# Wide silu columns, half-transfer semaphores and singly loaded modulation tiles at the start of a two-block transformer kernel

## The reference, cut to what matters

```python
mod_lat = split(silu(c) @ ada_w + ada_b, 6)          # six vectors of 1024, from one row c
a_lat = rmsnorm(x, g_pre) * (1 + mod_lat[1]) + mod_lat[0]
b_gate, c_gate, v = split(a_lat @ w_in, 3)            # w_in: 1024 x 3072
y_lat = (b_gate * depthwise_conv3(c_gate * v, conv_w)) @ w_out
x = x + mod_lat[2] * rmsnorm(y_lat, g_post)
f = square(relu(modulate(rmsnorm(x, g_pre_ff), mod_lat[3], mod_lat[4]) @ mlp_w_in)) @ mlp_w_out
x = x + mod_lat[5] * rmsnorm(f, g_post_ff)
# second block: rms norm, one wide projection, three branches (spatial gating, a convolution of
# 31 taps, stick-breaking attention), gates, an output projection, and a gated MLP with a
# convolution of 3 taps; the change does not touch it
```

## Time and profile before

| | us |
|---|---|
| median of 3 runs | 753.56 |
| range of the 3 runs | 753.12 to 753.70 |
| the profiled execution's own time | 754.83 |
| its span, first to last instruction | 753.1 |

### The profile page before, as it was taken

One profiled execution on the slowest core, in us unless ns is written; L12 is line 12 of the kernel. 1 busy time (PEld: TensorE's weight loads), 2 busy tenths in 40 slices (PEclk: granted clock), 3 DMA queues, 4 the chain that ended last, 5 costly groups with the idle time before them and its releaser, 6 DMA issues.

```text
span 753.1 us, 13240 instructions
## 1 busy us (share of the span) xinstructions
PE 746.7 (99%) x5352; PEld 694.9 (92%) x5352; DVE 553.0 (73%) x795; ACT 363.9 (48%) x453; POOL 12.1 (2%) x29
## 2 busy tenths in 40 slices
PE   8999999999999999999999999999999999999998
PEld 8889965999998888899979999999999999999998
DVE  4676998765665744489899976859779988887441
ACT  4125423755544333486555446584557554554330
POOL 0000000000000000020000001000000000000000
PEclk9899999999999999999999999999999999999999
DMA  9998998365565986545544252337453555443640
GB/s 302 349 345 317 352 359 311 117 242 183 192 183 181 341 260 195 199 151 210 183 168 168 81 197 102 119 133 265 170 222 121 216 180 203 157 134 127 207 139 28
DMA packets 53598, 152.68 MB, mean 203 GB/s; under 512 B 2928, under 2 KB 34032, under 8 KB 43312
## 3 DMA queue, kind: packets, MB, share of 16 engines
q1 hardware_dynamic: 52576, 149.43, 57.9%
q0 software_dynamic: 544, 1.84, 0.7%
q10 hardware_dynamic: 432, 0.76, 0.3%
HBM read 150.97 MB, written 1.05 MB: 202 GB/s over the span
## 4 chain that ended last, share of the span: by engine, by line
PE 88%; DVE 7%; ACT 3%; DMA 1%; issue 1%; SPq 0%; ACTq 0%; DVEq 0%
PE ps L1462 19%; PE ps L1464 19%; PE ps L1463 19%; PE ps L1543 6%; PE ps L1617 4%; PE ps L1618 4%; PE ps L1616 4%; PE ps L1663 4%; DVE w_lo L905 3%; DVE cacc L1236 2%; DMA raw<-in_ada 1%; ACT w_hi L539 1%; PE ps L1787 1%; PE ps L1785 1%; PE ps L1786 1%
## 5 line engine op out<-in xcount | busy, mean ns | idle before, releaser
L905 DVE TENSOR_TENSOR w_lo<-raw,w_hi 128x2048 fp32r<-128x2048 f32 (+2 forms) x116 | 246.0, 2122 | 85.0 <-ACT w_hi L539 84.9
L1462 PE MATMUL ps<-a_hi,w_hi 128*128 128x256 f32 x1024 | 290.7, 284 | 0.0
L1463 PE MATMUL ps<-a_lo,w_hi 128*128 128x256 f32 x1024 | 288.8, 282 | 0.0
L1464 PE MATMUL ps<-a_hi,w_lo 128*128 128x256 f32 x1024 | 288.4, 282 | 0.0
L539 ACT ACTIVATE w_hi<-raw 128x2048 fp32r<-128x2048 f32 (+2 forms) x116 | 205.8, 1778 | 99.6 <-PE ps L1618 44.0
L1462 PEld LDWEIGHTS ps<-a_hi,w_hi 128*128 128x128 f32 x1024 | 192.7, 188 | 1.3 <-issue 0.7
L1463 PEld LDWEIGHTS ps<-a_lo,w_hi 128*128 128x128 f32 x1024 | 192.7, 188 | 0.6 <-issue 0.5
L1464 PEld LDWEIGHTS ps<-a_hi,w_lo 128*128 128x128 f32 x1024 | 193.1, 189 | 0.0
L1462 PE MATMUL ps<-up_hi,w_hi 128*128 128x256 f32 x192 | 54.7, 285 | 0.0
L1463 PE MATMUL ps<-up_lo,w_hi 128*128 128x256 f32 x192 | 54.2, 282 | 0.0
L1464 PE MATMUL ps<-up_hi,w_lo 128*128 128x256 f32 x192 | 53.8, 280 | 0.0
(11 more groups left out here) (274 smaller groups left out, 939.7 us busy)
## 6 DMA issues: line engine op xcount, KB each, us to landing
raw<-in_w_z_in SPq DMA_DIRECT2D x26, 1024.0 KB, 4.8
raw<-in_w_up SPq DMA_DIRECT2D x22, 1024.0 KB, 4.7
raw<-in_w_mlp_in SPq DMA_DIRECT2D x16, 1024.0 KB, 5.0
raw<-in_w_mlp_out SPq DMA_DIRECT2D x16, 1024.0 KB, 5.8
raw<-in_w_down SPq DMA_DIRECT2D x16, 704.0 KB, 4.1
raw<-in_ada SPq DMA_DIRECT2D x16, 512.0 KB, 9.0
raw<-in_ada_half SPq DMA_DIRECT2D x8, 1024.0 KB, 7.9
raw<-in_ada SPq DMA_DIRECT2D x8, 1024.0 KB, 7.7
```

What stands on the lines that cost most here:

```text
L905: e.tensor_tensor(w_lo[:, slot, 0:words], raw[:, unit_slot, 0:words], w_hi[:, slot, 0:words].bitcast(f32), SUB).then_inc(raw_used, 1)
L1462: e.matmul(dst, w_hi[:, slot, cols], hi, start=start, stop=False, skip_group_check=skip)
L1463: e.matmul(dst, w_hi[:, slot, cols], lo, start=False, stop=False, skip_group_check=skip)
L1464: return e.matmul(dst, w_lo[:, slot, cols], hi, start=False, stop=stop, skip_group_check=skip)
```

## The change

It has five parts, and all of them lie ahead of or inside the products by key.

1. `shift_column(t, i)` is split in two halves i, of four products each, which wait for one half transfer. The moving operand is a `silu_c` column broadcast to 128 columns instead of one column, and the result lands in 128 equal columns of PSUM, of which `columns` reads the first. PE's order becomes tile 0 half 0, (wait for `x_r`) tile 1 half 0, tile 0 half 1, `tile_columns(0)`, tile 1 half 1, `tile_columns(1)`.
2. `part_in` has a semaphore for each half transfer. `pair_sum` starts on the first half, and takes the slices in the order of the halves.
3. The modulation units 2 and 3 no longer hold scale and shift of two tiles. `single_part(t)` loads both columns of feature tile t alone, in four DMAs of 256 KB with runs of 128 words (512 bytes) instead of 256 words. Unit 3 is issued after keys 1 instead of before them. `single_sum(t)` on DVE makes both sums in eight instructions of 128x2x128, and `tile_columns(2)` needs the third release only.
4. `par` is loaded in one DMA of 233 KB, behind the half of `x` on ACT's queue; before, its first 8 columns (the vector `c`) came first in a DMA of their own.
5. ACT loads silu's table first, then squares the first half of `x`, and evaluates `silu` after that.

```diff
+            def single_part(t):
+                for i in range(2):
+                    for v in range(2):
+                        at = (2 * i + v) * 512
+                        e.dma_start(raw[:, t, at:at + 512].rearrange("p (j f) -> p j f", j=4),
+                                    ada[4 * v:4 * v + 4].rearrange("j p (i f) -> i p j f", i=2)[i][:, :, t * P:(t + 1) * P])\
+                         .then_inc(part_in[t][i], 16)
...
             for q in range(4):
-                pair_part(2 * q)
-                pair_part(2 * q + 1)
+                if q == 1:
+                    single_part(2)
+                else:
+                    pair_part(2 * q)
+                    pair_part(2 * q + 1)
                 keys(q, 0)
                 keys(q, 1)
+                if q == 1:
+                    single_part(3)
...
-            e.dma_start(par[:, 0:8], params[:, 0:8]).then_inc(c_in_cols, 16)
             e.dma_start(x[:, 4:8, :], x_in[:, 4:8, :]).then_inc(x_landed[1], 16)
-            e.dma_start(par[:, 8:N_PARAMS], params[:, 8:N_PARAMS]).then_inc(par_in, 16)
-            e.wait_ge(c_in_cols, 16)
-            e.wait_ge(const_set, 1)
-            e.activation(silu_c[:, :], pcol("c", 0, 8), ACT.Silu).then_inc(c_ready, 1)
+            e.dma_start(par[:, :], params[:, :]).then_inc(par_in, 16)
+            e.preload_act_table_set("silu_and_others")
             e.wait_ge(x_landed[0], 16)
             e.activation(x_tok[:, 0, 0:512], flat(x[:, 0:2, :]), ACT.Square).then_inc(x_sq, 1)
+            e.wait_ge(const_set, 1)
+            e.wait_ge(par_in, 16)
+            e.activation(silu_c[:, :], pcol("c", 0, 8), ACT.Silu).then_inc(c_ready, 1)
...
+            def single_sum(t):
+                acc = pair_acc[:, 1, :, t % 2 * P:(t % 2 + 1) * P]
+                src = raw[:, t, :].rearrange("p (i v j f) -> p i v j f", i=2, v=2, j=4)
+                for i in range(2):
+                    e.wait_ge(part_in[t][i], 32)
+                    for j in range(4):
+                        col = silu_c[:, 2 * j + i:2 * j + i + 1]
...
-            pair_sum(1, 0)
-            pair_sum(1, 1)
-            for t in range(2, DT):
-                if t == DT - 1:
-                    a_low(0, 6)
-                columns(t)
-                if t < DT - 2:
-                    pair_sum(t // 2 + 1, t % 2)
+            single_sum(2)
+            columns(2)
+            single_sum(3)
+            columns(3)
+            pair_sum(2, 0)
+            pair_sum(2, 1)
+            columns(4)
+            pair_sum(3, 0)
+            columns(5)
+            pair_sum(3, 1)
+            columns(6)
+            a_low(0, 6)
+            columns(7)
...
-                e.wait_ge(raw_used, 1 if t < 2 else t // 2 * 2 + 2)
+                e.wait_ge(raw_used, (1, 1, 3, 4)[t] if t < 4 else t // 2 * 2 + 2)
...
-            def shift_column(t):
-                e.wait_ge(part_in[1], 32)
+            def shift_column(t, i):
+                e.wait_ge(part_in[1][i], 16)
                 e.wait_ge(c_ready, 1)
-                for k in range(DT):
-                    e.matmul(ps[:, column_bank(t), t:t + 1], src[:, k % 2, k // 2, t * P:(t + 1) * P], silu_c[:, k:k + 1],
-                             start=k == 0, stop=k == DT - 1)
+                for j in range(4):
+                    wide = silu_c[:, 2 * j + i:2 * j + i + 1].broadcast_to([P, P])
+                    e.matmul(ps[:, column_bank(t), P:2 * P], src[:, i, j, t * P:(t + 1) * P], wide,
+                             start=i + j == 0, stop=i + j == 4)
```

More of the change, by code:

```diff
@@ L253, in build_program @@
         x_new = sem("x_new")
-        part_in = [sem(f"part_in{i}") for i in range(PARTS)]
+        part_in = [[sem(f"part_in{i}_{h}") for h in range(2)] for i in range(PARTS)]
         key_in = [[sem(f"key_in{q}_{h}") for h in range(2)] for q in range(4)]
@@ L412, in pair_part @@
                                 ada[u % 2 * 4:u % 2 * 4 + 4].rearrange("j p (i f) -> i p j f", i=2)[i][:, :, u // 2 * 256:u // 2 * 256 + 256])\
-                     .then_inc(part_in[u], 16)
+                     .then_inc(part_in[u][i], 16)
+            def single_part(t):
[5 more added lines that the diff above has]
+                         .then_inc(part_in[t][i], 16)
             def keys(q, h):
@@ L925, in pair_sum @@
                 u = 2 * q + v
-                e.wait_ge(part_in[u], 32)
-                if u:
-                    e.wait_ge(raw_used, u)
                 acc = pair_acc[:, q % 2, v, :]
                 src = raw[:, u % RAW_SLOTS, :].rearrange("p (i j f) -> p i j f", i=2, j=4)
-                ch.link(e.tensor_scalar(acc, src[:, 0, 0, :], silu_c[:, 0:1], None, MUL))
-                for k in range(1, DT - 1):
-                    ch.link(ada_part(src[:, k % 2, k // 2, :], silu_c[:, k:k + 1], acc))
-                ada_part(src[:, 1, 3, :], silu_c[:, 7:8], acc).then_inc(raw_used, 1)
+                for i in range(2):
+                    e.wait_ge(part_in[u][i], 16)
+                    for j in range(4):
+                        col = silu_c[:, 2 * j + i:2 * j + i + 1]
+                        if i == 0 and j == 0:
+                            if u:
+                                e.wait_ge(raw_used, u)
+                            ch.link(e.tensor_scalar(acc, src[:, 0, 0, :], col, None, MUL))
+                        elif i == 1 and j == 3:
+                            ada_part(src[:, 1, 3, :], col, acc).then_inc(raw_used, 1)
+                        else:
+                            ch.link(ada_part(src[:, i, j, :], col, acc))
+            def single_sum(t):
+                acc = pair_acc[:, 1, :, t % 2 * P:(t % 2 + 1) * P]
+                src = raw[:, t, :].rearrange("p (i v j f) -> p i v j f", i=2, v=2, j=4)
+                for i in range(2):
+                    e.wait_ge(part_in[t][i], 32)
+                    for j in range(4):
+                        col = silu_c[:, 2 * j + i:2 * j + i + 1]
+                        if i == 0 and j == 0:
+                            e.wait_ge(raw_used, t)
+                            ch.link(e.tensor_scalar(acc, src[:, 0, :, 0, :], col, None, MUL))
+                        elif i == 1 and j == 3:
+                            ada_part(src[:, 1, :, 3, :], col, acc).then_inc(raw_used, 1)
+                        else:
+                            ch.link(ada_part(src[:, i, :, j, :], col, acc))
             def half_unit(k):
@@ L1045, in columns @@
                     ch.mark(plus)
-                ch.link(e.tensor_tensor(mod[:, one], ps[:, column_bank(t), one], pcol("ada_b", t), ADD))
+                shift = one if t > 1 else slice(P, P + 1)
+                ch.link(e.tensor_tensor(mod[:, one], ps[:, column_bank(t), shift], pcol("ada_b", t), ADD))
                 e.scalar_tensor_tensor(gain_pre[:, one], scale, 1.0, pcol("gains", t), ADD, MUL).then_inc(cols_ready, 1)
@@ L1544, in by_key @@
                 return mm
-            shift_column(0)
+            shift_column(0, 0)
+            e.wait_ge(x_r, 1)
+            shift_column(1, 0)
+            shift_column(0, 1)
             tile_columns(0)
-            e.wait_ge(x_r, 1)
-            shift_column(1)
+            shift_column(1, 1)
             tile_columns(1)
```

2 lines of the change are left out of this document (removed).

## The result

| | before | after |
|---|---|---|
| median of 18 runs each, in turn, us | 753.67 | 756.14 |
| lowest and highest, us | 753.12 to 755.43 | 753.66 to 757.44 |
| profiled execution, us | 754.83 | 755.36 |
| its span, us | 753.1 | 753.6 |
| its mean granted clock | 0.993 | 0.998 |

The ratio of the times is 1.0029, with a 95% interval of 1.0022 to 1.0037: the changed kernel is slower by 2.5 us. The mean granted clock of an execution sorts the 18 runs of after. At 1.000 it takes 753.66 us (one run), at 0.997 or 0.998 from 755.03 to 755.80 us (eight runs), at 0.995 from 756.49 to 757.44 us (nine runs).

What follows compares the result with a forecast made beforehand. PE's own work was taken as the bound. Of 5 us gained, the stall left 1.7; a clock fall of 2.3 made +0.6 us on the profiled 754.83, so 755.4 us, range 752.3 to 757.4 (8 in 10).

Steps and rivals of the forecast that it cites:

- The start: Ahead of the products by key: wide columns keep the clock full; first product at 17.2 us instead of 19.41.
- Parameters whole: Parameter load and ACT's start: `silu` moves from 5.59 to about 8.3 us, costing 0 to 0.3 us, taken as 0.2.
- Tiles 2 and 3 alone: Loads and sums of units 2 and 3: 3.6 us a unit; tile 3's columns at 32.3 us, 5 us gained so far.
- rival (b): Loads of units 2 and 3: small packets cost as much as large, 5.9 us a unit; 759 us; chance 0.06.
- The order on DVE: Ahead of tile 4's columns: two sums in a row stop PE for 3.3 us, leaving 1.7 of 5 us gained.
- The clock behind the stop: PE behind the stop ahead of tile 4's columns: the clock falls, costing 1.5 to 3.1 us, middle 2.3.
- From the profile to the median: Whole kernel: the profiled execution before is 1.27 us over its median, so medians differ by +1.9 us, giving 755.5.
- (a): PE's stop ahead of tile 4's columns: the clock holds through it, only the stall remains; 752.6 us; chance 0.20.
- (c): PE at the start: the clock falls near 15 us anyway; tile 4's columns at 45.7 us; some 757.5 us; chance 0.07.

Runs made afterwards that it cites:

- e3: The changed kernel with one silu column again as the moving operand instead of 128: 758.00 us, ratio to before 1.0055.
- e9: e1 with its 13 filling products cut to one moving column each: 755.54 us, ratio to before 1.0023.
- e4: The changed kernel with tiles 4 to 7 loaded and summed singly too: 752.14 us, ratio to before 0.9975.
- e1: The changed kernel with 13 dense 128x128 products added in PE's stop ahead of tile 4's columns: 753.64 us, ratio to before 0.9995.
- e8: e2 with the vector `c` in a DMA of its own again and `silu` ahead of the first square: 752.31 us, ratio to before 0.9978.
- e2: The changed kernel with units 2 and 3 again holding scale and shift of two tiles, as pairs: 751.55 us, ratio to before 0.9967.
- e5: e4 with those units read from a host-made copy in 4 KB runs, one 512 KB DMA per half: 750.22 us, ratio to before 0.9949.

## Why the prediction was right, step by step

- **The start.** The wide columns held the clock, and e3 and e9 show that it was the width. First product by key 17.2 us forecast, 17.25 measured; tile 2's columns 26.6 against 26.39. That it fits so closely is luck: in the profiles of e4, e9 and e1, with the same start, the first product comes at 17.51, 17.81 and 18.26 us.
- **Parameters whole.** Forecast as a cost of 0.2 us, by way of a later `silu`. In truth it is a gain. Between e8 and e2 this part is worth 0.8 us. After it `silu` runs at 7.39 us, not 8.3, since the DMA of 233 KB took 6.0 us instead of the 6.7 taken over from the earlier trace rows, and only the half of `x` stands ahead of it in its queue. This step failed, without weight in the sum. I had priced the consumers of `par`, and not what a small DMA does to the big ones behind it. The cost at the start is there (first product by key at 17.18 us in e2, 16.77 in e8), and the earlier transfers give back more. In after the sum for tile 3 waited for its unit too, so the same should hold there, but no run took this part out of after itself.
- **Tiles 2 and 3 alone.** 3.6 us for a unit forecast from the packet counts, 3.6 us measured by the rate (1.05 MB at 292 GB/s). "DMA: Bandwidth & Descriptors" of the Trainium skill (Specifications) puts line rate at 512 bytes and up; here 512-byte packets ran at 292 GB/s and longer ones at 349 and 387, so rival (b) is out, and so is that rule taken as full rate. Tile 3's columns are at 32.5 us against 32.3 forecast. Its sum ended 0.8 us later than my 31.7 us (28.46 + 4.0 = 32.5), since its first half was there at 28.4 us, and my landing times put it at 27.7 (25.9 + 1.8). The steps of the sum aren't the reason: all eight behind 27.7 us end at 31.7 too. By the DMA records unit 2 had landed at 20.7 us, earlier than my 21.4, but keys 1 and unit 3 took 9.4 us behind it instead of 8.1; why stays open.
- **The order on DVE.** 3.3 us of idle time forecast, 3.18 measured, tile 4's columns at 41.65 against 41.3 us. The columns are 0.35 us late, and a small piece was missing besides: PE's first columns behind a stop take 0.61 us and not 0.34. So what is left of the gain behind the stop is 43.01 + 0.34 - 41.65 - 0.61 = 1.1 us, where I had 1.7.
- **The clock behind the stop.** It fell, as forecast. 24 halves in 6.97 instead of 5.36 us are 1.6 us in the profile, where I had taken 2.3 from 1.5 to 3.1. The two misses cancel, by luck: -1.1 + 1.6 = +0.5 against the forecast's +0.6. In the medians the fall costs more, 2.5 us (after less e1), since in half of the executions the mean clock is 0.995 and not 0.998. The profile of e9 shows what such an execution looks like: 6.8 us at 0.50, a mean clock of 0.995 and 756.87 us. "TensorE: Matmul & The Clock Gate" of the Trainium skill, "HAM oscillation — how this bites in real kernels", has a wait between bursts put the next burst at half rate; after and e1 agree, with and without something in the gap.
- **From the profile to the median.** I had 1.9 us for the difference of the medians, and it is 2.5. The size of the part I took from before, its profiled execution being 1.2 us over its median, fits: -1.1 + 1.2 + 2.5 = 2.6 us. My reason for it, a slow clock that lasts longer in the profiled execution, isn't shown. The profiled one does have the lower mean clock (0.993), but executions of before at 0.995 take 753.1 to 753.8 us as well as 755.2 to 755.5.
- **Rivals.** (a) needs the clock to hold through the stop. One run of 18 did, at clock 1.000, and took 753.66 us; e1 forces it and takes 753.64. So its price, 752.6 us, was 1.0 too low: even then the change would have been no gain. (c) is out by the stretch of 15 to 30 us at clock 1.00.

Where the 5 us went, in the profiles: tile 3's columns came 4.8 us earlier. The stop took 3.2 us and the slower columns of tiles 3 and 4 behind their waits 0.27 us each, which leaves 1.1 us, and the clock took 1.6. Taken back step by step, in medians: the clock 2.5 us (after to e1), the order another 1.5 (e1 to e4, net of slower packets), larger packets and DMAs 1.9 (e4 to e5).

What stays open: why the low clock lasts 3.4 us in the profile of after and 6.8 us in that of e9, and why one execution of after kept its clock through the stop. The half-transfer semaphores and the order on PE weren't parted, nor packets and DMAs in e5.

## What to carry to other kernels

When a change brings one consumer forward, redraw the order of work on the engine that feeds it: two sums between two columns had cost nothing while PE was late, and cost 3.2 us and the clock once it was early. Fill a stop of TensorE that can't be avoided with dense, wide products, or don't have it; a stop's price is the idle time plus the slow clock behind it, and only the part not covered by a later wait counts. Signal each half transfer, and keep packets and DMAs large: the versions that do, and have no two sums between two columns once PE is early (e2, e5), beat both kernels.

## What the runs showed of the hardware

- An fp32 product with one moving column takes nearly as long as one with 128: 24 halves in 2.74 us (e3) and 2.84 us (after). It keeps PE busy, but the clock up in 3 of 11 executions only, against 11 of 11: 755.54 us (e9) against 753.64 (e1).
- With one stop of 3.2 us in otherwise dense products (after) the mean clock of an execution was below 1.000 in 17 of 18; with stops of 0.25 and 1.12 us (e2) it was 0.999 to 1.000 in all five; with stops of 1.32 and 1.09 us (e8) it was 1.000 in nine of 12 and 0.998 in three. In the profile of after the clock fell about 1 us behind the stop, and not in it.
- DMA rates on all 16 engines by packet: 292 GB/s at 512 bytes, 349 at 1 KB, 387 at 2 KB, 390 where part was at 4 KB (e5).
- A DMA of 4 KB at the head of ACT's queue moved the modulation units by 0.66 us, and the median of the kernel by 0.8 us (e2 to e8).
